# Two residual blocks on one core: three kinds of projection read their moved operand in two halves by turns

## The reference, cut to what matters

```
h = h + 0.5*swiglu(rms_norm(h, g1), w_ffn1_in, w_ffn1_out)
u = rms_norm(h, norm_mix);  proj = u @ w_in          # 1024 -> 4864
aq, ak, av, rq, rf, ri, rg, ga, gb = split(proj)
att = sliding_window_attention(aq, ak, av, ...)       # 8 heads, window 128
rec = hgrn2_recurrence(rq, rf, ri, lower_bounds)      # 4 heads of 128
merged = sigmoid(ga)*(att @ w_att) + sigmoid(gb)*(rec_normed @ w_rec)
h = h + merged @ w_out
h = h + 0.5*swiglu(rms_norm(h, g2), w_ffn2_in, w_ffn2_out)
h = h + sigmoid(rms_norm(h, g) @ w_ple_gate) * (p @ w_ple_proj)
# second block: a mixer (stick-breaking attention and RWKV-7), conv MLP, gate;
# then latent attention (c = hn @ w_down; q = norm(cq) @ w_uq; kv = norm(ckv) @ w_ukv),
# conv MLP, gate, final norm
```

## Time and profile before

| quantity | us |
|---|---|
| median of 3 runs | 1455.86 |
| the three runs | 1455.86, 1456.06, 1449.7 |
| profiled execution, device time | 1451.71 |
| its span from first to last instruction | 1450.0 |
| TensorE matmul busy | 1391.6 (96%) |
| TensorE weight load busy | 1322.6 (91%) |
| VectorE busy | 896.5 (62%) |
| ScalarE busy | 612.0 (42%) |
| GpSimd busy | 158.9 (11%) |

### The profile page before, as it was taken

One profiled execution on the slowest core, in us unless ns is written; L12 is line 12 of the kernel. 1 busy time (PEld: TensorE's weight loads), 2 busy tenths in 40 slices (PEclk: granted clock), 3 DMA queues, 4 the chain that ended last, 5 costly groups with the idle time before them and its releaser, 6 DMA issues.

```text
span 1450.0 us, 25626 instructions
## 1 busy us (share of the span) xinstructions
PE 1391.6 (96%) x10812; PEld 1322.6 (91%) x10812; DVE 896.5 (62%) x1191; ACT 612.0 (42%) x727; POOL 158.9 (11%) x149
## 2 busy tenths in 40 slices
PE   8999999899999999999999999999989999999997
PEld 8999999798899999888889879999988778999997
DVE  5766676674357665732485417877776774777675
ACT  5443454443134554421323522444454473444444
POOL 0000001141000000601020010000051060000023
PEclk9999999999999999999999979999999999999998
DMA  8555745332345555433410024555543503555530
GB/s 340 186 192 198 244 162 189 121 128 77 145 174 175 202 196 188 167 105 111 151 62 1 2 87 159 183 188 197 202 146 115 201 1 117 175 204 189 191 142 29
DMA packets 34744, 218.99 MB, mean 151 GB/s; under 512 B 4259, under 2 KB 6732, under 8 KB 9452
## 3 DMA queue, kind: packets, MB, share of 16 engines
q1 hardware_dynamic: 31888, 215.59, 41.9%
q10 hardware_dynamic: 2780, 2.30, 0.5%
HBM read 216.68 MB, written 1.06 MB: 150 GB/s over the span
## 4 chain that ended last, share of the span: by engine, by line
PE 81%; DVE 10%; ACT 3%; issue 2%; POOL 1%; DMA 1%; SPq 0%; ACTq 0%; POOLq 0%; DVEq 0%
PE ps L894 35%; PE ps L943 14%; PE ps L1034 6%; PE ps L847 6%; PE ps L1016 2%; DVE weights_second_parts L2330 2%; PE ps L1323 2%; PE ps L1328 1%; PE ps L859 1%; DVE x_second_part L2224 1%; PE ps L831 1%; PE ps L1105 1%; PE ps L1005 1%; ACT weights_first_parts L1641 1%; DMA weight_bays<-in_ffn_in 1%
## 5 line engine op out<-in xcount | busy, mean ns | idle before, releaser
L2330 DVE TENSOR_TENSOR weights_second_parts<-weight_bays,weights_first_parts 128x2048 fp32r<-128x2048 f32 x130 | 296.7, 2289 | 151.2 <-ACT weights_first_parts L1641 151.0
L1641 ACT ACTIVATE weights_first_parts<-weight_bays 128x2048 fp32r<-128x2048 f32 x130 | 249.1, 1924 | 260.9 <-PE ps L894 170.0
L894 PE MATMUL ps<-x_first_part,weights_first_parts 128*128 128x256 f32 x1472 | 197.2, 277 | 4.3 <-DVE weights_second_parts L2330 3.7
L894 PE MATMUL ps<-x_second_part,weights_first_parts 128*128 128x256 f32 x1472 | 196.2, 276 | 0.0
L894 PE MATMUL ps<-x_first_part,weights_second_parts 128*128 128x256 f32 x1472 | 196.0, 276 | 0.0
L894 PEld LDWEIGHTS ps<-x_first_part,weights_first_parts 128*128 128x128 f32 x1472 | 180.1, 192 | 5.7 <-ACT weights_first_parts L1641 2.6
L894 PEld LDWEIGHTS ps<-x_second_part,weights_first_parts 128*128 128x128 f32 x1472 | 180.8, 193 | 0.0
L894 PEld LDWEIGHTS ps<-x_first_part,weights_second_parts 128*128 128x128 f32 x1472 | 180.7, 192 | 0.0
L943 PE MATMUL ps<-hidden_first_part,weights_first_parts 128*128 128x256 f32 x704 | 136.5, 276 | 10.1 <-ACT weights_first_parts L1641 7.5
L943 PE MATMUL ps<-hidden_first_part,weights_second_parts 128*128 128x256 f32 x704 | 136.2, 275 | 0.0
L943 PE MATMUL ps<-hidden_second_part,weights_first_parts 128*128 128x256 f32 x704 | 136.1, 275 | 0.0
(11 more groups left out here) (429 smaller groups left out, 2191.1 us busy)
## 6 DMA issues: line engine op xcount, KB each, us to landing
weight_bays<-in_conv_in SPq DMA_DIRECT2D x44, 1024.0 KB, 4.7
weight_bays<-in_ffn_in SPq DMA_DIRECT2D x42, 1024.0 KB, 4.8
weight_bays<-in_ffn_out SPq DMA_DIRECT2D x22, 1024.0 KB, 4.8
weight_bays<-in_conv_out SPq DMA_DIRECT2D x22, 1024.0 KB, 4.7
weight_bays<-in_mix_in SPq DMA_DIRECT2D x19, 1024.0 KB, 4.8
weight_bays<-in_hyb_in SPq DMA_DIRECT2D x13, 1024.0 KB, 4.8
weight_bays<-in_ple_gate SPq DMA_DIRECT2D x12, 1024.0 KB, 4.7
weight_bays<-in_mix_out SPq DMA_DIRECT2D x4, 1024.0 KB, 5.3
```

What stands on the lines that cost most here:

```text
L894: mm = nc.tensor.matmul(dst, w[:, k, j * P:j * P + width], x[:, k], start=(n + k == 0), stop=(n == 2 and k == KD - 1))
L1641: nc.scalar.activation(hi, raw, ACT.Copy).then_inc(*w_hi_ready.inc(f, g, kind, of - g))
L2330: v.tensor_tensor(lo, raw, hi, ALU.subtract).then_inc(*w_lo_d.inc(f, g, kind, of - g))
```

## The change

The moved operand of the mixing, gate and latent projections is read through `in_halves` too. Where x is moved, the results lie in PSUM by turns and every instruction that reads them does so with a step of two. Where weights are moved (`ri`, `uq`, `ukv`), the host lays each row out with its even columns first, so that the reading by turns brings them back in order and the results are read as before. The halves are 128 elements apart at 256 columns and 256 elements apart at 512. The warm-up is 14 float32 matmuls, and the 24 float32r ones are gone. The diff, cut to its core:

```diff
-WARM = 8
+WARM = 14
...
+def evens_first(w, width):
+
+    w = w.reshape(-1, width)
+    return np.concatenate([w[:, 0::2], w[:, 1::2]], 1)
...
+    for n, (key, _) in enumerate(MIX_COLUMNS):
+        if key[0] == "ri":
+            out["mix_in"][n] = evens_first(out["mix_in"][n], 256).reshape(P, -1)
+    for name in ("uq", "ukv"):
+        out[name] = evens_first(out[name], 512).reshape(out[name].shape)
...
-    return t.rearrange("p k (a b) -> p k a b", a=2)
+    return t.rearrange("p (a b) -> p a b" if len(t.shape) == 2 else "p k (a b) -> p k a b", a=2)
...
-    return t.rearrange("p k (b a) -> p k a b", a=2)
+    return t.rearrange("p (b a) -> p a b" if len(t.shape) == 2 else "p k (b a) -> p k a b", a=2)
...
-        ones_r = ones[:].bitcast(F32R)
-        warm_patterns = [ones_r.rearrange("p (a b) -> p b a", a=2), ones_r, ones_r[:, 0:P], ones_r[:, 0:P].rearrange("p (a b) -> p b a", a=2),
-                         ones_r[:, 0:P + 64], ones_r[:, 0:P + 64].rearrange("p (a b) -> p b a", a=2)]
...
-            mixer_x = (mixer_hi, mixer_lo)
+            mixer_x = (in_halves(mixer_hi[:]), in_halves(mixer_lo[:]))
...
-                            mm = nc.tensor.matmul(ps[:, b, t * SEQ:(t + 1) * SEQ], x[:, k, t * P:(t + 1) * P], w[:, k],
+                            mm = nc.tensor.matmul(ps[:, b, t * SEQ:(t + 1) * SEQ], x[:, k, t * P:(t + 1) * P], in_halves(w[:, k]),
...
-                        mm = first_features(stage, dst, hi, lo, True, in_order)
+                        mm = first_features(stage, dst, hi, lo, True)
                     else:
-                        mm = split_features(dst[0], hi, lo, 0, in_order)
+                        mm = split_features(dst[0], hi, lo, 0)
...
-                        mm = split_features(dst[1], hi, lo, 1, in_order)
+                        mm = split_features(dst[1], hi, lo, 1)
...
-                                mm = nc.tensor.matmul(bank(UQ[n, t]), x[:, k, t * P:(t + 1) * P], w[:, k, :],
+                                mm = nc.tensor.matmul(bank(UQ[n, t]), x[:, k, t * P:(t + 1) * P], in_halves(w[:, k]),
...
-                                    mm = nc.tensor.matmul(bank(b), x[:, 3 + k, t * P:(t + 1) * P], w[:, k, half * 512:(half + 1) * 512],
+                                    mm = nc.tensor.matmul(bank(b), x[:, 3 + k, t * P:(t + 1) * P], in_halves(w[:, k, half * 512:(half + 1) * 512]),
...
-            for moving in warm_patterns:
-                for n in range(4):
-                    nc.tensor.matmul(ps[:, 7, 0:int(np.prod(moving.shape[1:]))], ones_r[:, 0:P], moving, start=True, stop=True)
...
-            def keep(dst, b, key, *event, c=slice(0, 512), func=ACT.Copy):
+            def keep(dst, b, key, *event, func=ACT.Copy):
 
                 act.wait_ge(*used_up_to(key))
-                src = ps[:, b, c]
-                if len(dst.shape) == 3:
-                    src = src.rearrange("p (a b) -> p a b", a=dst.shape[1])
+                src = ps[:, b].rearrange("p (a b) -> p a b", a=2)
+                if key[0] != "ri":
+                    dst, src = two_halves(dst), back_in_order(src)
                 nc.scalar.activation(dst, src, func).then_inc(*proj_a.inc(*event))
...
-                        ins = nc.scalar.activation(cl_hi[:, j], ps[:, n, j % 2 * SEQ:(j % 2 + 1) * SEQ], ACT.Copy, scale=gain)
+                        ins = nc.scalar.activation(two_halves(cl_hi[:, j]), back_in_order(ps[:, n, j % 2 * SEQ:(j % 2 + 1) * SEQ]), ACT.Copy, scale=gain)
...
-            def keep(dst, b, key, *event, c=slice(0, 512), scale=None):
+            def keep(dst, b, key, *event, scale=None):
                 dve.wait_ge(*used_up_to(key))
-                src = ps[:, b, c]
-                if len(dst.shape) == 3:
-                    src = src.rearrange("p (a b) -> p a b", a=dst.shape[1])
+                dst, src = two_halves(dst), back_in_order(ps[:, b].rearrange("p (a b) -> p a b", a=2))
...
-                v.tensor_copy(akT[:, 0], ps[:, 0, SEQ - 1::-1]).then_inc(*proj_d.inc("akT"))
-                v.tensor_copy(vT, ps[:, 0, 2 * SEQ - 1:SEQ - 1:-1]).then_inc(*proj_d.inc("akv"))
+                v.tensor_copy(two_halves(akT[:, 0]), back_in_order(ps[:, 0, 0:SEQ])[:, ::-1, ::-1]).then_inc(*proj_d.inc("akT"))
+                v.tensor_copy(two_halves(vT), back_in_order(ps[:, 0, SEQ:2 * SEQ])[:, ::-1, ::-1]).then_inc(*proj_d.inc("akv"))
...
-                    v.tensor_tensor(g, ps[:, 4 + n].rearrange("p (a s) -> p a s", a=2), by_token(rb[:]), ALU.mult).then_inc(*ple_d.inc(stage, n))
+                    v.tensor_tensor(two_halves(g), back_in_order(ps[:, 4 + n].rearrange("p (a s) -> p a s", a=2)), by_token(rb[:]), ALU.mult).then_inc(*ple_d.inc(stage, n))
...
-                        ins = v.scalar_tensor_tensor(cl_lo[:, j], ps[:, n, j % 2 * SEQ:(j % 2 + 1) * SEQ], gain, cl_hi[:, j], ALU.mult, ALU.subtract)
+                        ins = v.scalar_tensor_tensor(two_halves(cl_lo[:, j]), back_in_order(ps[:, n, j % 2 * SEQ:(j % 2 + 1) * SEQ]), gain, two_halves(cl_hi[:, j]), ALU.mult, ALU.subtract)
```

More of the change, by code:

```diff
@@ L848, in features @@
                 return mm
-            in_order, by_halves = (x_hi, x_lo), (in_halves(x_hi[:]), in_halves(x_lo[:]))
+            by_halves = (in_halves(x_hi[:]), in_halves(x_lo[:]))
             def first_features(f, dst, hi, lo, one_bank, xs=by_halves):
@@ L1973, in mla @@
                     tiles = range(2 * n, min(2 * n + 2, 5))
-                    nc.scalar.activation(mlsq[:, 2 * n:2 * n + len(tiles)], ps[:, n, 0:SEQ * len(tiles)].rearrange("p (a s) -> p a s", s=SEQ), ACT.Square)
+                    nc.scalar.activation(two_halves(mlsq[:, 2 * n:2 * n + len(tiles)]),
+                                         back_in_order(ps[:, n, 0:SEQ * len(tiles)].rearrange("p (a s) -> p a s", s=SEQ)), ACT.Square)
                     for j in tiles:
                         gain = col("q_norm", j) if j < 3 else col("kv_norm", j - 3)
-                        ins = nc.scalar.activation(cl_hi[:, j], ps[:, n, j % 2 * SEQ:(j % 2 + 1) * SEQ], ACT.Copy, scale=gain)
+                        ins = nc.scalar.activation(two_halves(cl_hi[:, j]), back_in_order(ps[:, n, j % 2 * SEQ:(j % 2 + 1) * SEQ]), ACT.Copy, scale=gain)
                     ins.then_inc(*lat_a.inc("c", n))
-                nc.scalar.activation(krT[0:32], ps[0:32, 3, 0:SEQ], ACT.Copy).then_inc(*lat_a.inc("kr"))
+                nc.scalar.activation(two_halves(krT[0:32]), back_in_order(ps[0:32, 3, 0:SEQ]), ACT.Copy).then_inc(*lat_a.inc("kr"))
                 def keep_turned(i):
@@ L2549, in ple @@
                     g, part = pgate[:, 6 + j], h[:, 6 + j]
-                    v.tensor_tensor(g, ps[:, b, 0:SEQ], rb[:], ALU.mult).then_inc(*ple_d.inc(stage, 3, j))
+                    v.tensor_tensor(two_halves(g), back_in_order(ps[:, b, 0:SEQ]), two_halves(rb[:]), ALU.mult).then_inc(*ple_d.inc(stage, 3, j))
                     dve.wait_ge(*ple_a.at(stage, 3, j))
@@ L2565, in scaled_embedding @@
                     e = emb[:, 2 * q:2 * q + 2]
-                    ins = v.tensor_tensor(e, e, by_token(rbe[:]), ALU.mult)
+                    ins = v.tensor_tensor(two_halves(e), two_halves(e), by_token(rbe[:]), ALU.mult)
                 ins.then_inc(*emb_d.inc(stage))
```

## The result

The changed kernel takes 1447.72 us in the median of 20 runs (1440.59 to 1453.0), the kernel before 1455.99 us in the median of 20 (1449.7 to 1459.65). The ratio is 0.9943, 95% interval [0.9927, 0.9958]: 8.3 us faster in the medians, 0.57%. 1446.3 was predicted, with a range of 1441 to 1454.

The account below looks back on a forecast made before the run. TensorE, busy for 1391.6 of 1450.0 us, was taken to bound the kernel. Mixing 4.2, gates 1.25 and latents 1.8 us summed to a gain of 7.3 us; 1446.3 us was named, range 1441 to 1454.

Parts of the forecast that it names:

- The rate: All changed matmuls: 118.0 ns falls to 111.7 at 256 columns, 6.3 ns each; ceiling with the 512-column ones 11.6 us.
- Chunks 0 to 8, 10, 11: Mixing stage: chunks 0 to 8 give 2.7 us, chunk 10 gives 0.3, chunk 11 nothing, ahead of 5.51 us of idle.
- Chunk 9: Mixing stage: its 0.3 us does not reach the end, since the scores wait for the DMA of the keys' halves.
- The loop: Mixing chunks 12 to 18: TensorE and a second circle tie at 7.5 us; 4 of 7 savings arrive, 1.2 us.
- The circle through ScalarE: In the loop: chunk's end, `keep`, first part, second part, L2478, L2479, then L1105 of the level after; 7.5 us.
- Gates: Three gate stages: 0.75 us in the first, 0.2 and 0.3 in the others; 1.25 us of a ceiling of 3.6.
- Latents: Latent projections: `down` 0.6 us, `uq` and `ukv` 1.2 us from 12.6 ns per matmul rounded down; 1.8 us in all.
- Warm-up: Kernel start: six more float32 matmuls cost nothing, or 0.5 us if they overran by one.
- ScalarE at a step of two: ScalarE's reads of PSUM: taken to cost nothing extra, with 0.43 us per tile as the upper bound.
- The rival of the clock: TensorE's clock: two to five new falls of 1.7 us each shrink the gain, giving 1450 to 1455; chance 0.07.
- The sign that I had named for a wrong forecast: TensorE's granted clock showing low stretches where it had none would mean the forecast is wrong.
- a frame of 1453.3: Whole kernel: the mean of all four executions before the change, from which the sum gives 1446.0 us.

Follow-up runs that it names:

- the first experiment: Changed kernel with twelve runs of 48 float32r matmuls added at its end, each in another operand order; 256 columns: in order 120.0 ns, halves 111.7.
- `after`: First profile of the changed kernel, nothing further changed; the profiled execution took 1449.56 us.
- `e5_changed_again`: The changed kernel run again with nothing altered, giving its second profile; 1449.2 us in the median of 12, ratio 0.9953 to the kernel before.
- `e3_probs_on_act`: Changed kernel with the softmax products moved from VectorE to ScalarE; 1448.99 us in the median of 10.
- `e4_loop_in_order`: Changed kernel with chunks 12 to 18 of the mixing stage read in order again; 1443.67 us in the median of 10.
- `e6_loop_order`: Changed kernel, softmax products on ScalarE, next level's exponential ahead of `keep`, its two VectorE products ahead of the second part; 1443.9 us, median of 6.
- filled run: Changed kernel with only filler matmuls added in TensorE's idle stretches; 1439.88 us in the median of 7 (1433.49 to 1444.45), ratio 0.9913.
- `e9_gates_alone`: Kernel before with the three gate stages alone read by turns; 1448.51 us in the median of 10, ratio 0.9969.

## Why the prediction was right, point by point

- **The rate.** Right: 111.7 ns in all the stages changed. What it rested on, one tile read in both orders, is what the first experiment shows, now beside four orders that are slower.
- **Chunks 0 to 8, 10, 11.** Right in each: the starts move by 0.30 us a chunk, chunk 11's goes into the 5.83 us. The DMA of the keys did start earlier with the chunks ahead, as the sum had it.
- **Chunk 9.** Right in the first profile, where its saving is the 0.31 us before L1090; in the second it arrives. In `after`, `e5_changed_again`, `e3_probs_on_act`, `e4_loop_in_order` and `e6_loop_order` the wait is 0.31, 0, 0.35, 0.24 and 0.15 us. The prediction kept this 0.3 us inside its range.
- **The loop.** The step that failed: "of each pair of savings one reaches the end: 4 of the 7 chunks, 1.2 us". The circle through ScalarE does span two steps, as it said: by the program the end of chunk 11+n leads to the L1105 ahead of chunk 13+n. But it took the stretch from the end of a chunk to L2479 for work of a fixed 7.5 us, with 2.73 for the second part and 0.68 for L2478, which took 1.60 in that very step. That stretch is not fixed: from the start of `keep` to the end of L2479 it is 7.3 us before (300.82 to 308.11) and 7.6 after (298.78 to 306.39), because the second part waits for GpSimd, and GpSimd's start hangs on L1105. What sets the step closes in every step and has no chunk in it, so the chunks 13 to 17 pass nothing on. Only chunk 12, ahead of the first such step, and chunk 18, behind which L1113 finds L2483 done 4 us before, give their 0.3 us. Measured 0.6. I named VectorE's L2479 as next late, which is right in place.
- **Gates.** Right; 1.55 us instead of 1.25. The third was priced 0.1 low.
- **Latents.** The size was off: 14 to 15 ns a matmul of 512 columns and not the 12.6 that go by columns, 1.46 us instead of 1.2. `down` was right.
- **Warm-up.** Priced at nothing, with 0.5 us for each float32 matmul where the earlier trace rows have 0.62; 0.2 us ahead when alone. The 0.4 and 0.8 us of the two profiles are partly the run's own.
- **ScalarE at a step of two.** Right at nothing: 592 ns.
- **The rival of the clock.** It holds in part. Both kernels lose 20 to 28 us of clock in a run, in places that change, and the change lengthened four idle stretches by 0.3 us. The sign that I had named for a wrong forecast, low stretches where there were none, did appear in the first profile; it says little, because such stretches move from run to run in every version. No run shows that the change made falls more frequent.
- **The number.** The sum, a gain of 7.3 us, is what the runs bear out: over all runs on record, the medians of the two kernels at an equal clock lie 7.1 us apart at 0.978, 7.3 at 0.981, 9.1 at 0.982 (two runs of the changed kernel) and 5.9 at 0.983 (one run). The 8.3 us of the medians have the luck of the clock in them, by my estimate 1 us, the 8.3 less some 7 at an equal clock. That 1446.3 came within 1.4 us of 1447.72 is partly luck too: it was taken from a frame of 1453.3, and the kernel before then had a median of 1455.99, from which the sum gives 1448.7. In the sum itself errors cancel: the loop 0.6 us too much, gates and latents 0.5 too little.

## What to carry to other kernels

Where one operand order is faster, count the savings to the first wait behind each run of matmuls: here 7.3 to 7.6 of 11.6 us arrived (the start left out), and most of what was lost is visible as waits grown by 0.3. For a loop that ties, write down every circle with the index of each event, and see over how many steps it closes. Check whether its terms are fixed: a helper's instruction that takes longer when it starts earlier is waiting for something, here for the other engine. In this loop the order of two instructions on VectorE was what mattered. And take those waits away afterwards: here that was worth 7 us at an equal clock, as much as the change (14.7 in the medians, half of it the clock's).

## What the runs showed of the hardware

- float32r matmuls of 256 columns: two interleaved streams 111.7 ns, one stream 118 to 120, four streams 143.5, pairs by turns 167, a step of eight 217.5, a step of two 226.5. The distance of the two halves (128 or 256 elements) does not matter at 512 columns (215.8 both).
- 128 columns take as long (110.6 ns) as 256 read by halves.
- VectorE and GpSimd hold each other up: L2123 takes 3.1 us beside L2307 instead of 1.07, and L2482 then 1.53 to 1.64 instead of 0.68. L2307 itself takes 2.28 us alone, and 2.6 to 3.2 when it starts beside GpSimd's L2122 or L2123; it ends 2.15 us behind the instruction of GpSimd that it met (302.13 and 304.28, 310.77 and 312.93).
- A run's mean granted clock ranges from 0.977 to 0.989 for one and the same kernel, which then takes 1455.0 and 1441.2 us (the one with the loop in order); one filled run had 0.995 and the second mixer at 1.00, where the changed kernel's profile shows 0.53 (`e9_gates_alone` has no low stretch there either).
